# Nine filler products behind the first MoE gather, and three VectorE steps re-ordered around it

## The chip, the cores and the metric

The kernel runs on one core of a Trainium2 chip. The metric is the device time of one execution, in microseconds (us), as the median of several runs. Five engines work beside each other: TensorE (PE in the profile; PEld is its weight load, PEldq its sequencer), VectorE (DVE), ScalarE (ACT), GpSimd (POOL) and SyncE (SP), which issues the loads. They meet through semaphores alone.

## The reference, cut to what matters

Two transformer blocks of two layers each over 256 tokens of width 1024, all in float32. What the change touches stands at the start of the first block's last layer, a mixture of eight experts with two chosen for each token:

```python
logits = (xf @ w_router).astype(jnp.float32)
top_logits, top_idx = lax.top_k(logits, TOP_K)
gates = jax.nn.softmax(top_logits, axis=-1)
...
def expert_block(args):
    tok, e = args
    xb = xf[tok]
    hb = jax.nn.silu(xb @ w_gate[e]) * (xb @ w_up[e])
    return hb @ w_down[e]
```

`gates` are called shares here. All but the few router rows of the work is dense products with weights that are read once.

## The kernel before

One instruction stream for each engine is written out by hand in Python (`tensor_program`, `vector_program`, `scalar_program`, `sync_program`, `pool_program`), and the order in the code is the order on the engine. Every weight unit of 1 MB is loaded by SyncE into one of six to nine slots (`raw`), ScalarE makes a rounded copy of it (`hi_to`, `whi`), VectorE the rest of that (`lo_to`, `wlo`, "a rest"), and TensorE multiplies three times for one float32 product: high by high, rest by high, high by rest (`natural`). `mark` raises a semaphore, `at` gives what to wait for.

The router stage goes as follows. TensorE turns the residual `x` and makes the logits. VectorE picks two experts per token (`chosen`). TensorE makes the ranks of the tokens within each expert in `bank[5]` (`pe_route`, L1631). VectorE copies the ranks (`posc`) and makes from them the one-hot matrices `S1` (`dve_hot`) and the largest count `cnt`. ScalarE makes `hh`, the normed `x` rounded, and VectorE its rest `hl` (`dve_hl`), in halves of 512 columns for each of the token blocks 0 and 1. TensorE gathers the tokens of the first two experts, `S1` with `hh` and `hl`, into banks 0 to 3 (`pe_gather_first`): 32 products of 256 columns. ScalarE takes them out of the banks as `xh` (`act_gather`, in the trace `low_hTh`), VectorE takes their rests `xl` (`dve_gather`, in the trace `low_hTl`), each in four quarters q.

Then comes a branch (`where_over`, L1886): each of the engines PE, ACT, DVE and SP waits for `cnt`, loads it into a register (L1893), and skips a long body for an expert with over 128 tokens by a compare-and-branch (L1894). With this data the body is skipped. Behind it stand the experts' steps: eight experts, seven chunks each, of gate, up and down products. The first product of expert 0 waits for `xl` of quarter 0, which serves the first two contraction tiles; each next quarter is wanted two tiles (six matmuls) later.

`pe_idle(e, n)` (L815) is n products of a 128x128 tile of ones with itself into bank 3, whose result nobody reads; each shows as two weight loads and two matmuls of the trace, `ps<-low_ones`. There are eight of them while TensorE waits for `chosen`, and five between the ranks and the gather.

Of the kernel before, what the change touches and what calls it, by code (L numbers as in the profile page):

```python
# [42 lines left out]
class Signals:  # L43
# [14 lines left out]
    def mark(self, name, *key, by=1):  # L58

        group = SEMAPHORE.get(name, name)  # L60
        n = self.count[group] = self.count.get(group, 0) + by
        if key:
            assert self.walked or (name, key) not in self.value, (name, key)
            self.value[name, key] = (name, n)
        return self.sem(name), by
# [5 lines left out]
    def at(self, name, *key):  # L71

        if not self.walked and (name, key) not in self.value:
            return self.sem(name), 1
        other, n = self.value[name, key]
        return self.sem(other), n
# [101 lines left out]
def two_block_kernel(nc, A, out):  # L178
# [9 lines left out]
    with ctx:  # L188
# [33 lines left out]
        ones = low("ones", [128, 128])  # L222
# [23 lines left out]
        def k(name, lo=0, n=None):  # L246
            a, b = COL[name]
            return col[:, a + lo:(b if n is None else a + lo + n)]

        bank = [ctx.enter_context(nc.psum_tensor(f"ps{i}", [128, 512], F32)) for i in range(8)]  # L250
        ACC, AB, TR = bank[0:4], bank[4:6], bank[6:8]
# [163 lines left out]
        def next_of(name, n=SPLITS):  # L415

            return split_units[min(named[name].s + n, len(split_units) - 1)]
# [5 lines left out]
        def lo_after(e, name, half=1):  # L423
            lo_to(e, next_of(name), half)
# [4 lines left out]
        def open_bank(e, b, *freed):  # L429


            for s in holds.get(b, ()):
                e.wait_ge(*at(*s))
            holds[b] = freed
            return bank[b]
# [376 lines left out]
            e.tensor_tensor(mTl[:, 0:4, s], blocks4(turns["hy_o", tb][:, :]), mTh[:, 0:4, s].bitcast(F32),  # L812
                            SUB).then_inc(*mark("hy_mTl", "o", tb))

        def pe_idle(e, n):  # L815

            for _ in range(n):
                e.matmul(ACC[3][:, 0:128], ones[:, :], ones[:, :], start=True, stop=True)

        def pe_hy(e):  # L820
            e.wait_ge(*at("const", "all"))
# [777 lines left out]
        def pe_gather_first(e):  # L1599


            for q in range(4):
                turns["gather", 0, q] = open_bank(e, q, ("xl", 0, q))
            e.wait_ge(*at("hot", 1))
            for tb in range(2):
                for q in range(4):
                    e.wait_ge(*at("hl", tb, q // 2))
                    for i in range(2):
                        s = slice(128 * (2 * q + i), 128 * (2 * q + i) + 128)
                        for z, h in enumerate((hh, hl)):  # L1610
                            t = e.matmul(bank[q][:, 256 * i:256 * i + 256], h[:, tb, s], S1[:, tb, 0:256],
                                         start=(tb, i, z) == (0, 0, 0), stop=(tb, i, z) == (1, 1, 1))
                    if tb:
                        t.then_inc(*mark("gathered", 0, q))
# [8 lines left out]
        def dve_gather(e, p, q):  # L1623
            xh, xl = xgs[p % 2]
            e.wait_ge(*at("xh", p, q))
            for i in range(2):
                t = e.scalar_tensor_tensor(xl[:, 2 * q + i, :], turns["gather", p, q][:, 256 * i:256 * i + 256],
                                           k("norm", 24 + 2 * q + i, 1), xh[:, 2 * q + i, :].bitcast(F32), MUL, SUB)
            t.then_inc(*mark("xl", p, q))

        def pe_route(e):  # L1631
            pe_router_x(e, 1, 0)
            pe_router_x(e, 1, 1)
            pe_router(e, 1, 0)
            pe_router(e, 1, 1)
            pe_idle(e, 8)
            P = open_bank(e, 5, ("ranks", "all"))
            e.wait_ge(*at("chosen", "all"))
            e.matmul(P[:, 0:16], strict[:, :], Mb[:, :, :].rearrange("p t e -> p (t e)"), start=True, stop=False)
            e.matmul(P[:, 8:16], onesb[:, :], Mb[:, 0, :], start=False, stop=True)  # L1640
            e.matmul(P[:, 16:24], onesb[:, :], Mb[:, 0, :], start=True, stop=False)
            e.matmul(P[:, 16:24], onesb[:, :], Mb[:, 1, :], start=False, stop=True).then_inc(*mark("sum", "ranks"))
            pe_idle(e, 5)
            pe_gather_first(e)

        def act_hT32(e, tb, n):
            e.wait_ge(*at("turned", "hT32", tb, n))
# [39 lines left out]
        def dve_hl(e, tb, n):  # L1687
            s = slice(512 * n, 512 * n + 512)
            e.wait_ge(*at("hh", tb, n))
            e.wait_ge(*at("rstd", tb))  # L1690
            e.scalar_tensor_tensor(hl[:, tb, s], x[:, tb, s], rs[:, 1, tb, 0:1], hh[:, tb, s].bitcast(F32), MUL,
                                   SUB).then_inc(*mark("hl", tb, n))
# [13 lines left out]
        def dve_route(e):  # L1706
            dve_residual(e, 3, 0, 0)
            dve_residual(e, 3, 0, 1)
            dve_rstd(e, 0)
            dve_hl(e, 0, 0)  # L1710
            dve_hl(e, 0, 1)
            dve_residual(e, 3, 1, 0)
            dve_residual(e, 3, 1, 1)
            dve_rstd(e, 1)

            e.wait_ge(*at("router", "all"))
            e.wait_ge(*at("sum", "logits"))
            e.tensor_copy(mL, AB[0][:, 0:16].rearrange("p (t e) -> p t e", t=2)).then_inc(*mark("logits", "all"))
            e.wait_ge(*at("logits", "all"))
            for tb in range(2):  # L1720
                e.max(mtop[:, tb, :], mL[:, tb, :]).then_inc(*mark("step"))
            e.wait_ge(*now("step"))
            for y in range(2):
                e.tensor_tensor(meq[:, y], mL, by8(mtop[:, :, y]), EQ).then_inc(*mark("step"))
            e.tensor_tensor(mnth[:, 1, :], mtop[:, :, 0], mtop[:, :, 1], EQ).then_inc(*mark("step"))
            e.wait_ge(*now("step"))
            e.tensor_tensor_scan(mcs.rearrange("p k t e -> p (k t e)"), d0[:, :, :, :].rearrange("p k t e -> p (k t e)"),
                                 meq.rearrange("p k t e -> p (k t e)"), 0.0, MUL, ADD).then_inc(*mark("step"))
            e.tensor_scalar(mnth[:, 1, :], mnth[:, 1, :], 1.0, None, ADD).then_inc(*mark("step"))
            e.wait_ge(*now("step"))  # L1730
            for y in range(2):
                e.tensor_tensor(mmask[:, y], mcs[:, y], by8(mnth[:, y]), EQ).then_inc(*mark("step"))
            e.wait_ge(*now("step"))
            e.tensor_tensor(mmask, mmask, meq, MUL).then_inc(*mark("step"))
            e.wait_ge(*now("step"))
            e.tensor_tensor(Mb[:, :, :], mmask[:, 0], mmask[:, 1], ADD).then_inc(*mark("chosen", "all"))
            e.tensor_tensor(mM, mmask[:, 0], mmask[:, 1], ADD).then_inc(*mark("step"))
            e.tensor_tensor(mdiff, mtop[:, :, 1], mtop[:, :, 0], SUB).then_inc(*mark("step"))
            e.wait_ge(*at("rstd", 1))
            e.wait_ge(*now("step"))  # L1740
            e.tensor_tensor(mdiff, rs[:, 1, :, 0], mdiff, MUL).then_inc(*mark("share", 0))
            e.wait_ge(*at("sum", "ranks"))
            e.tensor_copy(posc[:, :], AB[1][:, 0:24]).then_inc(*mark("ranks", "all"))
            also("places", ("all",), "ranks")
            e.wait_ge(*now("step"))
            e.wait_ge(*at("ranks", "all"))
            e.tensor_reduce(mmax, posc[:, 16:24], AX.X, MAX).then_inc(*mark("step"))
            dve_hot(e, 0)
            dve_hot(e, 1)
            e.wait_ge(*now("step"))  # L1750
            e.tensor_copy(cnt[:, :], mmax).then_inc(*mark("count", "all"))
            dve_hl(e, 1, 0)
            dve_hl(e, 1, 1)
            lo_after(e, "rg.o.2")
            e.wait_ge(*at("share_e", "all"))
            e.tensor_scalar(msum, mexp, 1.0, None, ADD).then_inc(*mark("step"))
            e.wait_ge(*now("step"))
            e.reciprocal(mrec, msum).then_inc(*mark("step"))
            e.wait_ge(*now("step"))
            e.tensor_tensor(mg2, mexp, mrec, MUL).then_inc(*mark("step"))  # L1760
            e.tensor_tensor(mt8, mmask[:, 0], by8(mrec), MUL).then_inc(*mark("step"))
            e.wait_ge(*now("step"))
            e.tensor_tensor(mG, mmask[:, 1], by8(mg2), MUL).then_inc(*mark("step"))
            e.wait_ge(*now("step"))
            e.tensor_tensor(mG, mG, mt8, ADD).then_inc(*mark("share", 1))
            for q in range(4):
                dve_gather(e, 0, q)
            lo_after(e, "rg.o.3")


# [1618 lines left out]
```

## Time and profile before

| | us |
|---|---|
| median of 3 runs | 2337.53 |
| lowest, highest | 2336.5, 2338.63 |
| the profiled execution's own time | 2337.59 |
| its span in the trace | 2335.8 |
| PE busy in the span | 2309.7 (99%) |
| DVE busy | 1797.4 (77%) |
| ACT busy | 1436.2 (61%) |

How to read it: the span is from the first to the last instruction of the trace, and 1.8 us of the execution lie outside it. Busy time of TensorE is modelled and its matmuls overlap, so a busy share near 99% says that it hardly ever waits, not that it is at its peak. The router stage and the branch lie between 424 and 445 us of the span, the experts behind them until about 1351 us.

### The profile page before, as it was taken

Reading aid. Unit: us, or ns where it says so; the run is one execution under the profiler, and the core shown is the slowest. Engines: PE = TensorE matmul, PEld = TensorE weight load, DVE = VectorE, ACT = ScalarE, POOL = GpSimd, SP = SyncE. Lnnn points to the kernel's source line nnn. Section 1 sums busy time; section 2 is a strip of 40 time slices with the busy share of each in tenths; the row PEclk is TensorE's granted clock in tenths of the full one; section 3 lists DMA queues with packets and bytes.
Section 4 is the critical chain, followed back from the end, with each engine's and each line's share of the span. In section 5 each row is a group of like instructions: output and inputs, shape, how many; then the busy total and the mean of one; then the engine's idle time right before and its main releaser. Section 6 shows DMA issues by size and latency. Waiting matters only on the chain.

```text
span 2335.8 us, 28884 instructions
## 1 busy us (share of the span) xinstructions
PE 2309.7 (99%) x11387; PEld 1910.6 (82%) x11387; DVE 1797.4 (77%) x2399; ACT 1436.2 (61%) x1985; POOL 7.8 (0%) x17
## 2 busy tenths in 40 slices
PE   9999999899999999999999999999999999999998
PEld 8888889788888888888888887777888877788887
DVE  7755558899989999999998999776755577767554
ACT  6444447677777777777777776554454464545443
POOL 0000000000000000000000000000000000000000
PEclk9999999999999999999999999999999999999999
DMA  8355555599999999999999997545555564455551
GB/s 286 127 198 181 180 180 179 212 344 364 359 363 349 375 356 363 351 377 361 348 363 376 359 362 223 181 153 181 171 192 179 180 222 130 155 195 174 198 181 54
DMA packets 266221, 588.93 MB, mean 252 GB/s; under 512 B 9440, under 2 KB 37360, under 8 KB 265824
## 3 DMA queue, kind: packets, MB, share of 16 engines
q1 hardware_dynamic: 265072, 581.82, 71.1%
q0 software_dynamic: 1008, 5.21, 0.8%
q8 instruction: 91, 1.49, 0.3%
q14 instruction: 50, 0.41, 0.1%
HBM read 585.92 MB, written 1.07 MB: 251 GB/s over the span
## 4 chain that ended last, share of the span: by engine, by line
PE 87%; DVE 9%; ACT 3%; issue 1%; DMA 0%; SPq 0%; DVEq 0%; ACTq 0%
PE ps L106 84%; DVE low_wlo L121 4%; PE ps L109 3%; ACT low_whi L115 1%; DVE s_rot L121 0%; ACT L112 0%; DVE low_nv L127 0%; DVE s_t L121 0%; ACT low_junk L112 0%; ACT s_p L112 0%; DVE s_sm L133 0%; DVE low_hTl L127 0%; DVE ffn_h L121 0%; DVE s_g L127 0%; DMA low_raw<-in_hy_w_in 0%
## 5 line engine op out<-in xcount | busy, mean ns | idle before, releaser
L121 DVE TENSOR_TENSOR low_wlo<-low_raw,low_whi 128x1024 fp32r<-128x1024 f32 (+1 forms) x992 | 1158.2, 1212 | 374.6 <-ACT low_whi L115 373.7
L115 ACT CAST low_whi<-low_raw 128x1024 fp32r<-128x1024 f32 (+1 forms) x992 | 984.6, 1043 | 386.9 <-PE ps L106 383.3
L106 PE MATMUL ps<-low_whi,low_hTh 128*128 128x512 f32 (+2 forms) x1616 | 631.0, 393 | 8.6 <-DVE low_wlo L121 3.6
L106 PE MATMUL ps<-low_whi,low_hTl 128*128 128x512 f32 (+2 forms) x1616 | 615.6, 384 | 0.0
L106 PE MATMUL ps<-low_wlo,low_hTh 128*128 128x512 f32 (+2 forms) x1584 | 605.9, 383 | 0.0
L106 PEld LDWEIGHTS ps<-low_whi,low_hTh 128*128 128x128 f32 x1616 | 304.5, 188 | 66.6 <-DVE s_g L127 3.8
L106 PEld LDWEIGHTS ps<-low_whi,low_hTl 128*128 128x128 f32 x1616 | 304.0, 188 | 60.4
L106 PEld LDWEIGHTS ps<-low_wlo,low_hTh 128*128 128x128 f32 x1584 | 298.8, 189 | 52.7 <-issue 0.5
L106 PE MATMUL ps<-low_whi,ffn_Th 128*128 128x512 f32 x608 | 243.4, 400 | 0.0
L106 PE MATMUL ps<-low_wlo,ffn_Th 128*128 128x512 f32 x608 | 237.2, 390 | 0.0
L106 PE MATMUL ps<-low_whi,ffn_Tl 128*128 128x512 f32 x608 | 194.3, 390 | 0.0
L106 PE MATMUL ps<-low_whi,moe_xh 128*128 128x512 f32 x448 | 174.7, 390 | 0.0
L106 PE MATMUL ps<-low_whi,moe_xl 128*128 128x512 f32 x448 | 174.3, 389 | 0.0
L106 PE MATMUL ps<-low_wlo,moe_xh 128*128 128x512 f32 x448 | 174.3, 389 | 0.0
L106 PEld LDWEIGHTS ps<-low_whi,ffn_Tl 128*128 128x128 f32 x608 | 114.1, 188 | 25.0
L106 PEld LDWEIGHTS ps<-low_wlo,ffn_Th 128*128 128x128 f32 x608 | 114.4, 188 | 21.8
L106 PEld LDWEIGHTS ps<-low_whi,ffn_Th 128*128 128x128 f32 x608 | 114.3, 188 | 21.7
L121 DVE TENSOR_TENSOR low_wlo<-raw,low_whi 128x1024 fp32r<-128x1024 f32 x102 | 120.1, 1221 | 7.4 <-ACT low_whi L115 7.4
L115 ACT CAST low_whi<-raw 128x1024 fp32r<-128x1024 f32 x102 | 102.0, 1050 | 20.1 <-PE ps L106 20.1
L106 PEld LDWEIGHTS ps<-low_whi,moe_xl 128*128 128x128 f32 x448 | 84.1, 188 | 17.5
L106 PEld LDWEIGHTS ps<-low_wlo,moe_xh 128*128 128x128 f32 x448 | 84.1, 188 | 17.2
L106 PEld LDWEIGHTS ps<-low_whi,moe_xh 128*128 128x128 f32 x448 | 84.1, 188 | 17.2
(359 smaller groups left out, 2318.4 us busy)
## 6 DMA issues: line engine op xcount, KB each, us to landing
low_raw<-in_moe_w_down SPq DMA_DIRECT2D x96, 1024.0 KB, 6.8
low_raw<-in_moe_w_gate SPq DMA_DIRECT2D x95, 1024.0 KB, 7.2
low_raw<-in_moe_w_up SPq DMA_DIRECT2D x94, 1024.0 KB, 6.8
low_raw<-in_w_ffn SPq DMA_DIRECT2D x66, 1024.0 KB, 5.1
low_raw<-in_w_in SPq DMA_DIRECT2D x28, 1024.0 KB, 5.4
low_raw<-in_w_merge SPq DMA_DIRECT2D x24, 1024.0 KB, 5.1
raw<-in_moe_w_up SPq DMA_DIRECT2D x18, 1024.0 KB, 7.0
raw<-in_moe_w_gate SPq DMA_DIRECT2D x17, 1024.0 KB, 7.2
```

The source lines that it names most:

```text
L106: return self.real.matmul(*a, **k) if self.real else WALK
L109: return self.real.transpose(*a) if self.real else WALK
L115: return self.real.copy(*a) if self.real else WALK
L121: return self.real.tensor_tensor(*a) if self.real else WALK
```

## The change

- `pe_idle` gets a third argument, the bank, 3 if not given.
- `pe_route` ends with nine more such products into bank 5, behind the gather's 32 matmuls and ahead of the branch.
- On VectorE `dve_hl(e, 1, 0)` moves from behind `cnt` to ahead of the wait for the ranks.
- `dve_gather` of quarters 0 and 1 moves from behind the shares to ahead of them; quarters 2 and 3 stay behind.

```diff
-        def pe_idle(e, n):
+        def pe_idle(e, n, b=3):
 
             for _ in range(n):
-                e.matmul(ACC[3][:, 0:128], ones[:, :], ones[:, :], start=True, stop=True)
+                e.matmul(bank[b][:, 0:128], ones[:, :], ones[:, :], start=True, stop=True)
...
             pe_idle(e, 5)
             pe_gather_first(e)
+            pe_idle(e, 9, 5)
...
             e.tensor_tensor(mdiff, rs[:, 1, :, 0], mdiff, MUL).then_inc(*mark("share", 0))
+            dve_hl(e, 1, 0)
             e.wait_ge(*at("sum", "ranks"))
...
             e.tensor_copy(cnt[:, :], mmax).then_inc(*mark("count", "all"))
-            dve_hl(e, 1, 0)
             dve_hl(e, 1, 1)
             lo_after(e, "rg.o.2")
+            dve_gather(e, 0, 0)
+            dve_gather(e, 0, 1)
             e.wait_ge(*at("share_e", "all"))
...
             e.tensor_tensor(mG, mG, mt8, ADD).then_inc(*mark("share", 1))
-            for q in range(4):
-                dve_gather(e, 0, q)
+            dve_gather(e, 0, 2)
+            dve_gather(e, 0, 3)
             lo_after(e, "rg.o.3")
```

## Rows read from the trace of the kernel before

**Rows 1.** Waits of TensorE, 445 to 1400 us: engine, line, releaser, us in total, times, longest.
```profile
PE ps L106 <- DVE low_hTl L127: 2.1, 1, 2.1
PE ps L109 <- DVE ffn_h L121: 0.3, 1, 0.3
```
**Rows 2.** Busy time in the experts' stretch (columns: us; PE, PEld, DVE, ACT, POOL; PEclk; DMA).
```profile
445.00:1351.00 906.00, 904.87 (x4126) 747.94 (x4127) 830.48 (x812) 693.19 (x776) 0.53 (x1) 1.00 0.99 358
```
**Rows 3.** Timeline of TensorE's matmuls: start, us, what, idle before and releaser.
```profile
438.30 0.50 PE L106 MATMUL ps<-low_ones 128*128 128x128 f32 x3
...
438.92 0.38 PE L106 MATMUL ps<-moe_S,moe_hh 128*128 128x256 f32 x1
...
442.74 0.28 PE L106 MATMUL ps<-moe_S,moe_hl 128*128 128x256 f32 x1
445.07 0.76 PE L106 MATMUL ps<-low_whi,low_hTh 128*128 128x512 f32 x1 [2.05 <-DVE low_hTl L127]
448.49 0.40 PE L106 MATMUL ps<-low_whi,low_hTl 128*128 128x512 f32 x1
```
**Rows 4.** The end of the program: TensorE's drain (line L3288), then its last matmuls.
```profile
L3288 PEldq DRAIN  x1: 4267/4267/4267, 2324.2 to 2324.2; - x1
...
2324.41 0.39 PE L106 MATMUL ps<-low_wlo,ffn_T 128*128 128x512 f32 x1
...
2328.03 0.39 PE L106 MATMUL ps<-low_whi,ffn_T 128*128 128x512 f32 x1
```
**Rows 5.** Busy time and granted clock by stretches (columns as in Rows 2).
```profile
444.00:445.00 1.00, 0.00 (x0) 0.00 (x0) 1.00 (x4) 0.98 (x3) 0.00 (x0) 0.96 0.79 233
445.00:446.00 1.00, 0.93 (x2) 0.83 (x3) 1.00 (x4) 0.99 (x2) 0.00 (x0) 0.50 1.04 397
```
**Rows 6.** Timeline of VectorE, 436 to 447 us.
```profile
436.66 0.16 DVE L121 TENSOR_TENSOR moe_sm<-low_rs,moe_sm 128x2 f32<-128x2 f32 x1
437.46 0.18 DVE L118 COPY moe_posc<-ps 128x24 f32<-128x24 f32 x1 [0.64 <-PE ps L106]
438.84 1.41 DVE L127 SCALAR_TENSOR_TENSOR moe_hl<-low_x,low_rs,moe_hh 128x512 fp32r<-128x512 f32 x2
442.43 0.17 DVE L124 TENSOR_SCALAR moe_sm<-moe_sm 128x2 f32<-128x2 f32 x1
443.42 3.22 DVE L127 SCALAR_TENSOR_TENSOR low_hTl<-ps,low_col,low_hTh 128x256 fp32r<-128x256 f32 x8
```
**Rows 7.** Line L103, the waits that stand alone, of TensorE's sequencer, 425 to 445 us.
```profile
L103 PEldq EVENT_SEMAPHORE  x1: 51/51/51, 445.0 to 445.0; - x1
```
**Rows 8.** Lines L1893 and L1894, the branch: duration ns min/median/max, first and last start us.
```profile
L1893 PEldq TENSOR_LOAD <-moe_cnt x1: 491/491/491, 440.7 to 440.7; - x1
L1894 PEldq COMPARE_BRANCH  x1: 3320/3320/3320, 441.6 to 441.6; - x1
L1894 ACTq COMPARE_BRANCH  x1: 45/45/45, 443.8 to 443.8; - x1
```
**Rows 9.** Timeline of ScalarE, 434 to 445 us.
```profile
434.91 1.34 ACT L112 ACTIVATE moe_hh<-low_x,low_rs 128x512 fp32r<-128x512 f32 x2
441.62 3.02 ACT L112 ACTIVATE low_hTh<-ps,low_col 128x256 fp32r<-128x256 f32 x8 [1.97 <-PE ps L106]
```
**Rows 10.** TensorE's instruction fetches (DMA queue q8), at 442.5 to 442.7, 446.5 to 447, 457 to 458.
```profile
q8 instruction: 1, 0.02, 27.8%
...
q8 instruction: 1, 0.02, 12.9%
...
q8 instruction: 1, 0.02, 5.8%
```
**Rows 11.** Tile `ones`: duration ns min/median/max, first and last start us.
```profile
L106 PE MATMUL ps<-low_ones x58: 274/363/579, 1.3 to 438.8; 128*128 128x128 f32 x58
```
**Rows 12.** The chain that ended last, 455 to 475 us, in order of time.
```profile
457.80 0.69 DVE ffn_h L121
...
472.12 0.66 PE ps L109 x4
```

## The prediction

> **What bounds the kernel now.** I read the page first: TensorE is busy 99% of the span. The second view is TensorE's waits in the experts' part: from 445 to 1400 us there are only two, 2.1 us at the very start and 0.3 us once [rows 1], and it is busy 904.87 of 906 us [rows 2]. So a microsecond won or lost ahead of the first expert moves everything behind it one for one, and the whole change lies ahead of it. The third view is the timeline of TensorE at that place [rows 3]. The last gather matmul starts at 442.74, the first expert matmul at 445.07; the array is idle for 2.05 us and then runs cold: from 445.07 to 448.49 it starts eight matmuls, 0.43 us apart, where matmuls of this kind at full clock start 0.226 us apart (16 steps from 2324.41 to 2328.03) [rows 4]. Eight at 0.226 would be 1.8 us, and they took 3.42: 1.6 us lost. The granted clock says the same: 0.96 over the microsecond from 444, so it fell at about 444.9, after 1.9 us without work, and 0.50 over the next [rows 5]; 1.00 and 0.50 are the levels of 2.4 and 1.2 GHz. The place is therefore worth 2.05 + 1.6 = 3.65 us, or 0.16% of the kernel, and no edit here can win more than that.
>
> **What the 2.05 us wait for.** This decides the sign. The waits name VectorE's `low_hTl` as releaser [rows 1]. But its eight steps start at 443.42 and take 3.22 us [rows 6], 0.40 each, and the first matmul wants only the first two: ready at 443.42 + 0.80 = 444.2, or 0.8 us before TensorE starts. The separate wait in front of the first expert matmul lasts 51 ns [rows 7], the time of a wait that is already met. What does end at the right moment is the branch: PE's compare-and-branch begins at 441.6 and lasts 3.32 us, until 444.93, the wait stands at 445.0, the matmul at 445.07 [rows 7, 8]. ScalarE's branch took 45 ns, and it went through at 443.8 while its engine still worked until 441.62 + 3.02 = 444.64 [rows 8, 9], so a branch does not wait until its engine is empty. What sets PE's apart: its skipped body is thousands of instructions long, and one instruction fetch of its queue lies at 442.5 to 442.7, 0.9 us after the branch began, the next at 446.5 [rows 10]. I read the 3.3 us as the cost of reaching code that is not loaded. It counts from the branch's own start, not from the gather's end.
>
> The Trainium skill (Runtime: NRT & Kernel Launch, "Instruction fetch mechanics") says that a taken branch to a page outside the two that are loaded must fetch that page before anything goes on; the trace agrees in kind with its 3.32 us, and the rule speaks against putting work ahead of the branch.
>
> **The nine products.** They are 18 matmuls and 18 weight loads. At full clock three of the existing ones take 0.50 us with a duration of 0.27 each, so they start within 0.23 us, 0.115 us each [rows 3, 11]; 18 x 0.115 = 2.07 us. They run from about 442.86 to 444.93 and cover the old gap. The question is where the branch goes. It stands behind them in the stream, and the sequencer can only be so far ahead of the array. Two rows show how far: `cnt`'s register load begins at 440.7 with 17 gather matmuls still to start (0.12 us apart up to 442.74) [rows 3, 8], and the drain at the end of the program begins at 2324.2 with again 17 matmuls still to start, from 2324.41 to 2328.03 [rows 4]. The same number at two different paces (0.12 and 0.226 us) reads as a limit of the queue, 17 pairs. Then the branch starts when 17 of the 50 matmuls remain, so exactly 18 matmuls later than before: +2.07 us. Register load and branch take as long as before (0.94 + 3.32 us). Branch end: 444.93 + 2.07 = 447.0; first expert matmul 447.14; idle from 444.95 to 447.1, again 2.1 to 2.2 us. The bounds of this term: 0, if the branch's end never mattered, and +2.2 with 0.12 us for each matmul. I take 2.07.
>
> **VectorE's order.** `dve_hl(1,0)` needs `hh`, whose first half is there at 434.91 + 0.67 = 435.6 [rows 9]. It starts at 436.8 behind the product for the shares and takes 0.70 us (1.41 for two) [rows 6], until 437.5, while VectorE was idle for 0.64 us until 437.46. So the copy of the ranks comes 0.0 to 0.1 us later; I take 0.05, and it moves the one-hots, the gather and all behind by as much. What is queued behind it on VectorE is just that chain, and TensorE waits for it under five filler products, which end when they end. The time that it leaves, 0.65 us, lets `hl(1,1)` end at 439.6 for 440.25 and the weight rest behind it as much earlier, but the gather never waited for `hl` (its 32 matmuls stand 0.12 us apart from 438.92 to 442.74) [rows 3], so nothing is gained there. SyncE's next load, which waits for that weight rest, goes out 0.6 us earlier; TensorE has no wait for a load in the 900 us behind [rows 1], worth 0.
>
> **Quarters ahead of the shares.** ScalarE's quarters take 3.02/4 = 0.755 us each from 441.62 [rows 9]: ready at 442.4, 443.2, 443.9 and 444.65. VectorE would take quarter 0 at 442.45 to 443.25 and quarter 1 until 444.05, then the shares (442.43 to 443.42, so 1.0 us) until 445.05, then quarters 2 and 3 until 446.7. Quarter 0 comes 0.95 us earlier, quarters 2 and 3 as before. With the first matmul at 447.1 all four lie ready, so this edit is worth 0 under the forecast; it pays only if data and not the branch held TensorE. If TensorE started at 445.0, quarter 2 would be wanted 12 matmuls on, at 447.7, and is there. Nothing new becomes late.
>
> **The clock.** The array idles 2.1 to 2.2 us where it idled 2.05 us, ahead of the same expert matmuls, so I charge the same cold stretch, 1.6 us: difference 0. Its bounds are -1.6 (the products keep the clock up) and +1.6 (one more cold stretch behind the later gap).
>
> **Does it pass through?** In the first expert step VectorE works almost without a pause from 457.80 to 472.1 and TensorE waits 0.3 us for it [rows 1, 12]. That run starts with TensorE's own sum of the step, so it moves with TensorE, and the delay stays whole.
>
> **Sum.** +2.07 + 0.05 + 0 + 0 = +2.1 us. The profiled execution took 2337.59 (span 2335.8 and 1.8 around it), 0.06 above the median of the three runs, so both give the same base: 2337.6 + 2.1 = **2339.7 us**.
>
> **The rivals.**
> (a) *Data held TensorE, as the waits view has it.* Then the branch's 3.32 us are only the wait for `xl`, and moving quarter 0 ahead plus filling the gap does what the change says. First expert matmul at 445.0 (products end 444.93, `xl` ready 443.3), -0.05 us, and with no gap no cold stretch, -1.6: 2336.0. Against it stand the 51 ns wait and the fetch at 442.5; for it the releaser named, and that the fourth `low_hTl` step ends within 0.1 us of TensorE's start.
> (b) *The sequencer is not limited to 17 pairs.* Then the load at 440.7 was held by `hl(1,1)`, ready at about 440.2, with 16 instructions behind it in 0.45 us, so 0.028 us each. Now `hl(1,1)` is there at 439.6; from the release at 438.97 the gather's 64 and the fillers' 36 instructions go out in 2.8 us, load at 441.8, branch end 446.05, first expert matmul 446.2. The gap shrinks to 1.2 us, +1.1, and if that is too short for the clock to fall, -1.6: net -0.5 or 2337.1; with the fall 2338.7. Against it: the same 17 at the program's end, though two equal numbers can be chance, which is why it keeps nearly a fifth.
> The Trainium skill (TensorE: Matmul & The Clock Gate, table at the head) gives TensorE's queue a depth of 64, above the 34 instructions of my reading; by it the result would be that of (b).
> (c) *Slower: a second fetch.* The 36 new instructions shift the branch's target within its loaded block. If it lands so near the block's end that TensorE eats the rest (two instructions in 0.23 us) before the next fetch is there, a second stall of 3.3 us adds to the first: 2339.7 + 3.3 = 2343.0. It decides below about 29 instructions left in the block. In the trace the fetches behind the branch come at 446.5 and then only between 457 and 458 [rows 10]; 12 us at that pace are some 100 instructions, so 36 fewer are still enough.
> (d) *The products don't show at all in the time*, with gains and losses under 0.5 us: 2337.6; any mixture of (a), (b) and the forecast.
>
> **How the numbers follow.** Forecast +2.1: 0.52, of which one extra cold stretch (2341.3) 0.07. Rival (a) 0.17, (b) 0.18, (c) 0.04, (d) 0.09. A measurement of this kernel can tell about 0.2%, 4.7 us, from no change. Only (c) passes that bound, with the extra cold stretch near it: slower 0.05. A gain of 4.7 us is more than the place holds (3.65); I leave 0.02 for something unseen; same 0.93. The range of 8 in 10 goes from a little below (a), for the 1 us by which runs differ, to a little over the extra cold stretch: 2335.3 to 2341.8.
>
> **What would show it.** Right: PE's register load of `cnt` at about 442.8 and the branch's end at 447.0; no work of TensorE between 445.0 and 447.1; clock at half behind it; `low_hTl` in two groups with the shares between, the first ending at about 444.1. Wrong: the expert matmul at 445.0 with full clock (rival a), a register load at 441.8 (rival b), or two long fetch gaps (rival c).

## The result and the profile after

The changed kernel takes 2344.75 us (median of 8 runs, 2341.39 to 2346.31), the one before 2337.22 us (8 runs, 2335.55 to 2338.63): ratio 1.0029, 95% interval 1.0020 to 1.0039. That is 7.5 us slower, by more than a measurement of this kernel can tell from no change, where 2.1 us were forecast; the time lies 3 us above the range.

The branch lines of the changed kernel (L1896 and L1897 answer to L1893 and L1894 of [rows 8]; duration ns, then start us):

```profile
L1896 PEldq TENSOR_LOAD <-moe_cnt x1: 481/481/481, 445.9 to 445.9; - x1
L1897 PEldq COMPARE_BRANCH  x1: 5188/5188/5188, 446.8 to 446.8; - x1
L1897 ACTq COMPARE_BRANCH  x1: 45/45/45, 446.8 to 446.8; - x1
```

TensorE's matmuls (answering to [rows 3]): the gather's first and last, the products, the first expert matmul:

```profile
441.95 0.39 PE L106 MATMUL ps<-moe_S,moe_hh 128*128 128x256 f32 x1 [0.85 <-DVE moe_cnt L118]
...
445.77 0.28 PE L106 MATMUL ps<-moe_S,moe_hl 128*128 128x256 f32 x1
445.89 2.17 PE L106 MATMUL ps<-low_ones 128*128 128x128 f32 x18
452.12 0.47 PE L106 MATMUL ps<-low_whi,low_hTh 128*128 128x512 f32 x1 [4.06 <-DVE low_wlo L121]
```

The 18 matmuls run as costed. The register load begins with the first of them, 17 before the end. But the branch behind it lasts 5.19 us for 3.32, until 451.96, and TensorE stands still for 4.06 us where it stood for 2.05. The releaser that the row names, a weight rest of VectorE, is not what released it: the separate waits in front take their 51 ns each, as in [rows 7], and in e7 below, the same kernel without the branch, the experts start 1.8 us before VectorE begins that rest (444.20 and 446.02):

```profile
L103 PEldq EVENT_SEMAPHORE  x4: 51/51/51, 452.0 to 452.4; - x4
```

VectorE's moved steps (answering to [rows 6]): the half `hl(1,0)` stands between the choice of the experts and the copy of the ranks, and two quarters of the gathered rows' rests (x4) ahead of the shares, two behind:

```profile
439.39 0.18 DVE L121 TENSOR_TENSOR moe_Mb<-moe_sm 128x16 bf16<-128x16 f32 x1
...
439.84 0.74 DVE L127 SCALAR_TENSOR_TENSOR moe_hl<-low_x,low_rs,moe_hh 128x512 fp32r<-128x512 f32 x1
440.50 0.17 DVE L118 COPY moe_posc<-ps 128x24 f32<-128x24 f32 x1
...
445.53 1.66 DVE L127 SCALAR_TENSOR_TENSOR low_hTl<-ps,low_col,low_hTh 128x256 fp32r<-128x256 f32 x4 [0.64 <-ACT low_hTh L112]
...
448.07 1.65 DVE L127 SCALAR_TENSOR_TENSOR low_hTl<-ps,low_col,low_hTh 128x256 fp32r<-128x256 f32 x4
```

What happened to the fetch begins in SyncE's timeline, where the 1 MB load is issued at 444.92:

```profile
444.92 0.37 SPq L145 DMA_DIRECT2D low_raw<-in_moe_w_gate  x1
```

In the stretches of the same trace (columns as in [rows 2]) its packets fill the DMA engines until about 449.5. The last row is from the experts' first microseconds, with the granted clock at 0.50:

```profile
446.00:447.00 1.00, 1.00 (x11) 1.00 (x10) 1.00 (x4) 1.00 (x4) 0.00 (x0) 1.00 0.75 139
447.00:448.00 1.00, 1.00 (x10) 0.87 (x8) 0.86 (x7) 0.98 (x3) 0.00 (x0) 1.00 1.04 371
448.00:449.00 1.00, 0.06 (x1) 0.00 (x0) 1.00 (x4) 0.99 (x2) 0.00 (x0) 1.00 1.05 406
449.00:450.00 1.00, 0.00 (x0) 0.00 (x0) 1.00 (x3) 0.20 (x1) 0.00 (x0) 1.00 0.40 141
...
454.00:455.00 1.00, 1.00 (x4) 0.72 (x4) 0.00 (x0) 0.00 (x0) 0.00 (x0) 0.50 0.91 336
```

TensorE's instruction fetch of 445.75 to 446 comes before the branch starts; the next one lies at 449.25 to 449.5, as the load's packets end. It starts 2.7 us after the branch began, where it was 0.9 us in [rows 10] (the instruction queue's row of the DMA view, in either stretch; its last figure is the fetch's own time as a share of 16 engines' stretch, so 27.5% of 4 us is 1.10 us):

```profile
q8 instruction: 1, 0.02, 33.7%
...
q8 instruction: 1, 0.02, 27.5%
```

All 16 traces that have the branch fit one sum (starts and times from the trace's own records, finer than the views print): the time from the branch's start to the start of the last fetch inside it, plus that fetch's own time, plus 1.4 to 1.5 us until the branch ends. For the trace before it is 0.93 + 0.89 + 1.50 = 3.32 us, for the changed kernel 2.66 + 1.10 + 1.42 = 5.19.

**The run in parts.** A trace is cut here at three starts: the step that chooses the experts (`moe_Mb`, up to which all kernels run the same instructions), the gather's first matmul, the first expert matmul. The rest is the span less the last of these. The label before with a number is the kernel before traced again, after with a number the changed one.

| trace | choice at | to the gather | gather to experts (middle part) | rest | branch, us |
|---|---|---|---|---|---|
| before | 436.29 | 2.63 | 6.15 | 1890.7 | 3.32 |
| before_2 | 435.86 | 1.98 | 6.21 | 1889.1 | 3.32 |
| before_3 | 436.67 | 2.64 | 6.15 | 1890.6 | 3.32 |
| before_4 | 438.88 | 2.68 | 6.52 | 1889.1 | 3.70 |
| after | 439.39 | 2.56 | 10.17 | 1890.7 | 5.19 |
| after_2 | 437.59 | 2.68 | 10.06 | 1892.0 | 5.09 |
| after_3 | 438.66 | 2.76 | 10.16 | 1891.8 | 5.17 |
| after_4 | 437.96 | 2.72 | 10.25 | 1891.9 | 5.19 |

Means of four: 436.9, 2.5, 6.3, 1889.9 before and 438.4, 2.7, 10.2, 1891.6 after. The difference of 7.3 us is 1.5 ahead of the choice, 0.2 between choice and gather, 3.9 in the middle part and 1.7 behind. The 3.9 is by far the steadiest, and the experiments are mostly about it.

### The profile page after: what moved, and what is told of

It is laid out like the page before. It is cut to its first block, busy times and chain, and to the rows that moved or that the text cites. A ratio compares the mean times of both kernels' runs of the same rounds, so it can differ in the third digit from the quotient of the medians.

```text
span 2342.8 us, 28920 instructions
## 1 busy us (share of the span) xinstructions
PE 2315.2 (99%) x11405; PEld 1915.2 (82%) x11405; DVE 1797.1 (77%) x2399; ACT 1436.8 (61%) x1985; POOL 7.8 (0%) x17
## 4 chain that ended last, share of the span: by engine, by line
PE 87%; DVE 9%; ACT 3%; issue 1%; DMA 0%; DVEq 0%; SPq 0%; ACTq 0%
PE ps L106 84%; DVE low_wlo L121 4%; PE ps L109 4%; ACT low_whi L115 1%; DVE s_rot L121 0%; DVE low_hTl L127 0%; DVE low_nv L127 0%; ACT L112 0%; DVE s_t L121 0%; ACT s_p L112 0%; DVE s_sm L133 0%; DVE ffn_h L121 0%; ACT low_junk L112 0%; DVE s_g L127 0%; DVE rg_qs L130 0%
```

## The experiments

The theory as it stood after the result, called the branch theory: TensorE's branch releases the experts; it begins when 17 matmuls are left in the queue; its fetch comes late when a weight load is under way. The main rivals: data (VectorE's rests) releases them; the target's place in its block of instructions makes the branch long; cold stretches elsewhere make the difference.

**e1_order_only: VectorE's order alone.**

```diff
             pe_gather_first(e)
-            pe_idle(e, 9, 5)
```

> The change without the nine products: only VectorE's order is changed. Branch theory (TensorE's branch starts when 17 matmuls are left in its queue, its end releases the experts, and its fetch takes longer when a weight load is under way): the branch starts as before, about 2.8 us after the gather's first matmul, its fetch comes out ahead of the load's packets, so it lasts 3.3 us, and from the gather's first matmul to the first expert matmul it is 6.15 us as before; time within 0.5 us of before. Data theory (the rests of the first quarter release the experts): that distance shrinks by 0.8 us, and if the clock then stays up another 1.6 us go: 0.8 to 2.4 us faster. If the moved steps on VectorE are what costs, it is slower by some of the 7 us.

Measured: 2338.51 us, ratio 1.0003 (0.9994 to 1.0012). Middle part 6.47 us though the first quarter of rests was ready 4.44 us after the gather's first matmul, for 5.37 before; rest 1889.2. The branch lasted 3.66 us, more than the 3.3 expected. The branch, then the load in SyncE's timeline:

```profile
L1896 PEldq COMPARE_BRANCH  x1: 3657/3657/3657, 444.0 to 444.0; - x1
```

```profile
444.33 0.37 SPq L145 DMA_DIRECT2D low_raw<-in_moe_w_gate  x1
```

Data does not release the experts: with data earlier they start no earlier. The order alone costs at most what the interval allows, 2.8 us, and the difference can't be told from none.

**e2_fillers_only: the products alone.** As the change, with VectorE's order of before.

```diff
             pe_gather_first(e)
+            pe_idle(e, 9, 5)
```

> The kernel before with only the nine products behind the gather. Branch theory: the branch starts 18 matmuls later (2.1 us), its fetch then meets the 1 MB weight load issued at the gather's end and it lasts about 5.2 us for 3.3: 4 to 5 us from the first gather to the first expert matmul more than before, and the whole 7 us of the change or nearly so. Data theory: the experts start where they did or earlier, since the products only fill the gap; 1.6 us faster if the clock stays up. If cold stretches elsewhere in the run make the difference and not the place of the change, this kernel and the one without the products scatter alike around the kernel before.

Measured: 2343.87 us, ratio 1.0027 (1.0016 to 1.0037). The products alone bring nearly the whole loss, 6.3 us by the ratio. Middle part 12.31 us and a branch of 7.19 us, both 2 us more than expected. The branch, the load's issue in SyncE's timeline, and the instruction queue in the DMA view of 447.5 to 447.75 us:

```profile
L1895 PEldq COMPARE_BRANCH  x1: 7185/7185/7185, 444.6 to 444.6; - x1
```

```profile
443.29 0.37 SPq L145 DMA_DIRECT2D low_raw<-in_moe_w_gate  x1
```

```profile
q8 instruction: 2, 0.03, 102.0%
```

Two instruction fetches stand in that last stretch at once, as the load ended; their own times are 1.33 and 2.75 us, and the branch ends 1.38 us after the longer one. Of the changed kernel's traces, after has one fetch ahead of the load's packets and one behind them, after_2 one 0.7 us into them and one behind; after_3 and after_4 show only the one behind. I read the extra 2 us of e2 as two fetches that share the way behind the load; one trace shows it, and why the other kernels have one fetch there stays open.

**e3_load_held and e9_fillers_held: the same two kernels with the load out of the way.** The edit on the changed kernel is e3, on e2 it is e9:

```diff
+                if u.before is named["e0.g0.1"]:
+                    e.wait_ge(*at("xl", 0, 3))
                 e.dma_start(u.raw, u.src)
```

> The whole change, but SyncE holds the one weight load that is under way during the branch until the last quarter of rests is made. If the fetch behind the branch is slowed by that load, the branch lasts 3.3 us again and the first expert matmul comes 1.9 us earlier than in the changed kernel, so the time is about 2 us below the changed kernel and the gap over the kernel before shrinks to 2 us plus what the clock takes. If the longer branch comes from where its target lies in its block of instructions, it lasts 5.2 us as before and nothing changes. A held load can itself cost at most what its later landing delays, and no engine waited for a landing in this part.

> The nine products with VectorE's order of before (as e2_fillers_only, whose branch lasted 7.19 us), and the weight load of that moment held until the last quarter of rests is made. If a load in the way of the fetch made the branch long there, it lasts 3.3 to 4.0 us here, the first expert matmul comes 8.3 to 8.9 us after the gather's first for 12.31, and the time is 2 to 4 us below e2's. If the branch's length comes from where the target lies in its block of instructions (the same in both kernels but for the shift of no instruction), it stays at 5 to 7 us.

Measured: e3 2341.58 us, ratio 1.0016 (1.0007 to 1.0025), middle part 8.94; e9 2340.46 us, ratio 1.0011 (1.0002 to 1.0020), middle part 8.76. Their branch rows, e3's first, then the fetch inside the branch for e3 (DMA view of 445.0 to 445.25), e9 (447.0 to 447.25) and before_4 (445.0 to 445.25):

```profile
L1899 PEldq COMPARE_BRANCH  x1: 3970/3970/3970, 444.0 to 444.0; - x1
```

```profile
L1897 PEldq COMPARE_BRANCH  x1: 3785/3785/3785, 446.1 to 446.1; - x1
```

```profile
q8 instruction: 1, 0.02, 38.7%
...
q8 instruction: 1, 0.02, 31.5%
...
q8 instruction: 1, 0.02, 32.0%
```

5.2 us became 3.97, 7.19 became 3.79, and both medians fell by over 3 us against the kernel with the load under way. Of e3's 3.2 us its trace has 1.2 in the middle part and 1.0 in the rest (1890.6 for 1891.6 on average, a shorter cold stretch); of e9's 3.4 us the middle part alone has 3.55. Neither kernel moves an instruction of TensorE against its partner, so it is the load and not the target's place. What is left in the middle part over the 6.15 us of before, 2.8 and 2.6 us, is the later branch (2.1) and 0.65 and 0.5 us of a branch that is still longer than 3.32. The last rows place that piece: with the load held the fetch starts 1.0 us after the branch again, but takes 1.55 us in e3 and 1.26 in e9 where it took 0.88 to 0.91 in three traces of before. before_4 (branch 3.70) has 1.28, e1 (3.66) 1.08. Why a fetch is longer with no load in its way stays open.

**e8_fillers4: four products.** `pe_idle(e, 4, 5)` in the changed kernel.

> The whole change with four products for nine. Branch theory: the branch begins 8 matmuls later than without products (0.9 us) and not 18 (2.1 us), with 17 matmuls still to start; its fetch asks 1.1 us earlier against the load than in the changed kernel, about as the load's packets begin, so it lasts 3.5 to 5 us. Middle part 7.2 to 8.9 us (6.15 with none, 10.1 with nine); time 2 to 4 us below the changed kernel. If the nine products only had to be fewer to be free, the middle part is 6.2 us.

Measured: 2343.35 us, ratio 1.0026 (1.0017 to 1.0036). A miss: the middle part is 10.06 us where 7.2 to 8.9 were expected, the same as with nine. TensorE's sequencer, then the load in SyncE's timeline:

```profile
L1896 PEldq TENSOR_LOAD <-moe_cnt x1: 488/488/488, 442.5 to 442.5; - x1
...
L1897 PEldq COMPARE_BRANCH  x1: 6220/6220/6220, 443.3 to 443.3; - x1
```

```profile
442.71 0.37 SPq L145 DMA_DIRECT2D low_raw<-in_moe_w_gate  x1
```

The branch starts earlier, as the queue of 17 has it (at 442.5 nine gather matmuls and eight of the products are still to start), and lasts just as much longer; the fetch lies at 447.0 to 447.25 in the trace's DMA view. So between four and nine the number of products doesn't set the price; the load does. From its issue to the end of the branch it is 7.0 us in the changed kernel (444.92 to 451.96; 6.9, 7.0 and 7.0 in the other three traces) and 6.9 us here (442.71 to 449.57). Four products are already enough to put the fetch behind the whole megabyte; with fewer nothing was run.

**e6_no_branch and e7_no_branch_after: no branch on any engine**, in the kernel before and in the changed one.

```diff
+            return
             v = e.real.value_load(cnt[0:1, 0:1], min_val=0, max_val=SEQ)
```

> The kernel before without the branch on any engine (no register load, no skipped body; the handling of an expert with over 128 tokens is left out, which this data does not need). Branch theory: the first expert matmul comes when the first quarter is there, 5.35 us after the gather's first matmul for 6.15, and nothing stands still later: 0.8 us faster, up to 2.4 if the clock stays up. Data theory: the first expert matmul stays 6.15 us behind, same time.

> The whole change without the branch on any engine (the handling of an expert with over 128 tokens is left out, which this data does not need). If position ahead of the branch is all that is wrong with the products, the experts start as soon as the products end, 6.0 us after the gather's first matmul, with no gap of TensorE and the clock at full: 6 to 8 us faster than the changed kernel, 1 to 2 us faster than before, and within 1 us of the kernel without branch and products, which has a gap of 1.3 us there. If products cost in another way (the clock, a bank, a slower weight load), a gap or a cold stretch stays.

Measured: e6 2337.17 us, ratio 0.9997 (0.9988 to 1.0007), middle part 5.42; e7 2336.43 us, ratio 0.9996 (0.9987 to 1.0005), middle part 5.87, rest 1889.1. First the first expert matmul of e6, then that of e7:

```profile
445.98 0.50 PE L106 MATMUL ps<-low_whi,low_hTh 128*128 128x512 f32 x1 [1.33 <-DVE low_hTl L127]
```

```profile
444.20 0.48 PE L106 MATMUL ps<-low_whi,low_hTh 128*128 128x512 f32 x1
```

In e6 VectorE's rest is the releaser in truth (ready at 5.36 us, experts at 5.42), 0.7 us ahead of where the branch let the experts start. In e7 the products do what they do on paper: no gap, clock at full, and the time is 8.3 us below the changed kernel. Against the kernel before no gain can be told from none; the interval allows up to 3 us, so the 1 to 2 us expected are neither shown nor ruled out.

**e4_branch_late, e5_late_order4, e10_change_late: the branch behind the 24 gate matmuls.** e4 is the kernel before with this move, e5 has besides VectorE's order with all four quarters ahead of the shares, e10 the whole change.

```diff
             pe_route(e)
-            where_over(e, pe_overflow)
...
+                if c_ == 0:
+                    where_over(e, pe_overflow)
                 for q in pe_gate_up(e, c_, "u", 1, "mprod"):
```

> The kernel before with TensorE's branch moved behind the 24 gate matmuls of the first expert step (512 columns each), the other engines' branches where they were; the skipped body then uses banks 0 and 1 in place of 4 and 5. Branch theory: the first expert matmul now comes when the first quarter of rests is made, about 0.8 us earlier (5.35 us after the gather's first matmul), and 17 queued matmuls at 0.226 us cover 3.8 of the 4.3 us that the register load and the branch take, so TensorE stands still for 0.5 to 1 us at the branch, up to 2.5 us if a load slows the fetch; in sum between 0.5 us faster and 1.5 us slower than before, and up to 1.6 us faster again if the clock stays up. Data theory: the first expert matmul doesn't move and the branch costs nothing at either place.

> TensorE's branch behind the 24 gate matmuls as in e4_branch_late, VectorE's order of the change, but all four quarters of the gathered rows' rests ahead of the shares, no filler products. In e4 the register load began only when the last quarter was there, 13 matmuls ahead of the array and not 17; here the last quarter comes 1 us earlier. Branch theory: first expert matmul 4.5 us after the gather's first (6.15 before, 5.42 in e4), the register load with 17 matmuls still to start, TensorE idle for 0.7 to 1.2 us at the branch (1.4 in e4) and 1.4 us ahead of the experts for 2.05: 0.7 to 2 us faster than before by the gaps, 1.6 more in runs in which the clock stays up. Rival: the queue holds whatever the branch needs and TensorE's gap at the branch stays at 1.4 us or grows with a load in the fetch's way: same time as before.

> The whole change, nine products and order, with TensorE's branch behind the 24 gate matmuls (banks 0 and 1 in the skipped body). If the place ahead of the branch is what makes the products cost, the middle part is 5.9 us with no gap (as in the kernel without any branch), the gap at the branch is 1.4 to 1.8 us, the clock stays up at the experts' start in every run, and the time is within 1 us of the kernel before, 7 us below the changed kernel. If the products cost by themselves, it stays several us above the kernel before.

Measured: e4 2337.79 us, ratio 1.0004 (0.9995 to 1.0013), middle part 5.42; e5 2336.56 us, 0.9999 (0.9990 to 1.0008), 4.49; e10 2338.74 us, 1.0009 (1.0000 to 1.0018), 5.86. e4's gap at the branch is 1.38 us, where 0.5 to 1 was expected without a load in the way. The gap of e5 and then of e10:

```profile
450.52 0.50 PE L106 MATMUL ps<-low_whi,low_hTh 128*128 128x512 f32 x1 [1.50 <-issue]
```

```profile
452.76 0.50 PE L106 MATMUL ps<-low_whi,low_hTh 128*128 128x512 f32 x1 [1.05 <-DVE low_wlo L121]
```

The change that costs 7.5 us with the products ahead of the branch costs 1.6 us by the medians with the branch moved (1.0 more than e4), so some 6 us of the loss hang on the products' place ahead of the branch. e5 has the lowest median of the kernels that keep the branch, but its ratio cannot be told from 1: it wins 1.7 us ahead of the experts and gives 1.5 us back at the branch, where 0.7 to 1.2 were expected. In e5 the register load began at 445.63 with 14 matmuls to start, not 17 (14 in e4 too), since it waited for the last quarter of rests, ready at 445.57. No run takes the skipped body, so that it still works with its banks exchanged is not shown.

**before_2 to before_4, after_2 to after_4: more traces of the two kernels.**

> The kernel before, unchanged, for a second trace. Its time is cut into three parts: up to the gather's first matmul, from there to the first expert matmul, and the rest. In the first trace they were 438.92, 6.15 and 1890.73 us. Branch theory: the middle part is again 6.1 to 6.6 us with a branch of 3.3 to 3.7 us, and the rest is 1890.7 or, where the clock stays up behind the gap, 1889.1. The first part ranges from 438 to 442 us by the cold stretches that fall into it, in this kernel as in the changed one. Rival: the first part of the kernel before is always near 439 and that of the changed kernel near 442, so that part of the loss is made ahead of the place of the change.

> The changed kernel, unchanged, for a second trace. Its first one gave 441.95, 10.17 and 1890.68 us for the three parts, with a branch of 5.19 us. Branch theory: middle part 8.5 to 12.5 us, set by a branch of 3.3 to 7.2 us whose fetch meets the load, begun as the products begin; rest 1890.7 us, always with the cold stretch, since the gap is long every time; first part anywhere from 438 to 442 us. Rival: first part near 442 us again.

> The kernel before, unchanged, a fourth trace. Up to the step that chooses the experts all kernels run the same instructions; in three traces of before that step starts at 435.9 to 436.7 us, in three of the changed kernel at 437.6 to 439.4 us, in the others from 435.8 to 439.3 us. If that is luck of the clock (cold stretches at 50 and at 416 us), this trace falls anywhere from 435.8 to 439.4; if it belongs to the kernel, near 436.3 us.

The single times were 2334.96, 2337.92 and 2339.01 us, and 2344.17, 2345.32 and 2344.55. before_4 starts its choice at 438.88, so a late start is not the changed kernel's own; e6 and e9, both without VectorE's order, had 438.58 and 439.31, and e7, which has the whole change but the branch, 435.78. The late ones go with stretches at half clock near 50 and 416 us, where nothing was edited. Yet all four traces of the changed kernel are at 437.6 or later, against four of the other fourteen. Whether that is more than chance stays open, and with it about 1.5 of the 7.5 us.

## Why the prediction was wrong, point by point

**What bounds.** Right: the branch, not the rests that the waits view names. e1, e6, e7 and the 51 ns waits show it; rival (a) falls.

**The nine products.** The 18 matmuls at 0.115 us and the 17 pairs ahead held: the register load stands at the first product in the changed kernel, at 17 matmuls to go in e8 too, as in all 13 traces in which no wait held it. Rival (b) falls. The +2.07 us is in the middle part.

**The length of the branch: the step that failed.** "Register load and branch take as long as before (0.94 + 3.32 us)" took the 3.32 as a constant. The register load's part held (0.86 us in the traces of both kernels, a little under the 0.94). But the branch holds an instruction fetch, and that shares the DMA engines with the weight loads. In the kernel before the fetch at 442.5 slipped through because the load was issued only at 442.55 and its packets began at 443.58; the trace had these numbers. Two microseconds later it stood behind the whole load. The branch took 5.1 to 5.2 us for 3.32: +1.8 us in the changed kernel, and 3.9 in e2. Held load and moved branch (e3, e9, e10) take this back. Rival (c) forecast a second stall behind the branch from where the target lies; no trace shows one.

**SyncE's load.** I gave its 0.6 us earlier issue the value 0, asking only who waits for its data. It has another side: the load is issued 2.97 us after the gather's first matmul for 3.63, nearer to the fetch. With a free way the fetch comes about 1 us after the branch starts, the load's packets about 1 us after its issue, so what counts is which of branch and issue comes first: before, the branch begins 0.97 us ahead of the issue, in e1 0.3 us, in e8 0.6 us behind. In the changed kernel this earlier issue is not what does the harm: e2 has the old issue, 1.3 us ahead of its branch, and its fetch falls behind the load all the same.

**VectorE's order.** +0.05 us holds at best where the clock is down there: 2.6 to 2.8 us with the old order, 2.55 to 3.0 with the new. With the clock up, choice to gather is 1.98 us with the old order (before_2, e4, e6, e9) and 2.55 with the new (after, e7): +0.57. The trace that I read had a cold stretch just there, which made TensorE the late one and hid the half of `hl`.

**The clock.** "The same cold stretch, difference 0" was mis-sized by 1.7 us on average. Behind a gap of 2.1 to 2.4 us the first expert matmuls were cold in two traces of before and warm in two (rest 1890.7 or 1889.1); behind 4 us they were cold in all four, and in three of these for longer: after_2 starts some 14 expert matmuls 0.43 us apart, where before starts eight. The bound of +1.6 named this, the chance given to it (0.07) looks too small: three traces in four of the changed kernel have it.

**The rest.** That the delay goes through whole was right: in the traces of the two kernels the rest is 1889.1 us with no cold stretch, 1890.6 to 1890.7 with one of eight matmuls and 1891.8 to 1892.0 with one of 13 or 14. The Trainium skill (Runtime: NRT & Kernel Launch, "Instruction fetch mechanics") has a taken branch stall until the page of its target is fetched, where that is not loaded; the traces agree, and what a run adds is 3.3 to 7.2 us by what else is on the DMA engines. The Trainium skill's queue depth of 64 for TensorE (TensorE: Matmul & The Clock Gate, table at the head) is not what these runs show: 17 matmuls with their 17 weight loads were ahead each time that no wait held the sequencer, and the measurement decides.

## What to carry to other kernels

Work put ahead of a far branch to fill a gap moves the gap: ask first what ends the wait, by the sequencer's own rows, and whether it counts from the work that you add. A duration that contains a fetch is no constant; look at which load is issued around it (here 1.85 us ahead of the branch did the harm, 0.97 us behind it did little). And a step "hidden" by an engine that runs at half clock in the one trace at hand must be costed again with that engine at full clock.

## What was not expected of the hardware

- A branch over thousands of instructions stops TensorE for 3.32 us (three traces alike), 5.1 to 5.2 us with a 1 MB load issued 1.8 us ahead of it, 7.2 us in one trace with two fetches behind the load. ScalarE's and VectorE's branches took 0.045 and 0.072 us each time.
- In 16 traces such a branch ends 1.4 to 1.5 us after the last fetch inside it; what varies is when that fetch starts (0.9 to 3.8 us after the branch) and its own time (0.88 to 1.55 us, 2.75 with two at once).
- With the load ahead and one fetch behind it, the branch ends 6.9 to 7.0 us after the load's issue, whether it begins 0.6 or 1.85 us after it.
- The sequencer of TensorE was ahead of the array by 17 matmuls and their weight loads, with 256 columns, 512 columns and 128x128 float32 products alike, unless a wait held it back.
